# Memory keys and values of the cross attention as split products with rounded operands, the value weights in blocks of 256 outputs

## The chip, the cores and the metric

The kernel runs on one core of a Trainium2 chip. The metric is the device time of one execution in microseconds (us); before and after are compared by the median of several runs. The engines are TensorE (PE, its weight loads PEld), VectorE (DVE), ScalarE (ACT), GpSimd (POOL) and the queue of SyncE (SP), which issues nearly all transfers.

## The reference

Two networks run one after the other on the same 512 tokens of width 1024, all in float32. The first has two hybrid layers (convolution, grouped attention, a gated recurrence, a Fourier mix) and ends with an RMS norm. The second begins with that result as its stream x and has a memory of 256 rows:

```python
x = first_block(...)                                  # 512 x 1024
h = _rms_norm(x, g_mix_pre)
proj = h @ w_in                                       # 22 tiles of 128 columns and a narrow one
...                                                   # window attention, gated delta net, w_out
c = _memory_cross_attention(_rms_norm(x, g_cross_pre), _rms_norm(mem, g_mem), w_cq, w_ckv, w_co)
x = x + _rms_norm(c, g_cross_post)
f = _swiglu(_rms_norm(x, g_ffn_pre), w_gate_up, w_down)
```

The keys and the values of the cross attention are `_rms_norm(mem, g_mem) @ w_ckv`: a 256 x 1024 matrix times 1024 x 1024 for the keys and the same for the values. They don't depend on x, and the kernel computes them between the two networks.

## The kernel before

Activations lie feature-major: tile k of `h` holds features 128 k to 128 k + 127 on the partitions and tokens along the row, 512 latent ones (`LAT`) and behind them 256 (`CTX`) which hold the memory rows (`mem_x`) once the last layer of the first network no longer needs them. All weights stream through a ring of five chunks of 128 x 1024 (`ring`), one transfer each, in one fixed order. A chunk is normally all that one output tile of 128 features needs. A transfer into a place of the ring waits until PE has used the chunk five before it (`chunk_used`).

Nearly every projection is a split product (`project_split`, L1568 to L1589). A weight chunk is rounded to the format fp32r by ACT into one of two buffers (`w_lead`, in the table of names `scratch_r`; L668), then POOL subtracts the rounded part from the chunk in place (L507, `w_split`). The activations are split in the same way (rounded part and rest) by DVE, ACT or POOL. PE then makes three products of rounded operands per tile: first part by first part, first part by rest, rest by first part. ACT may write the rounded part of chunk m only when PE is done with chunk m - 2:

```python
if m >= 2:
    act.wait_ge(chunk_used, SPLIT_STREAM[m - 2] + 1)
```

The memory keys (`ck`) and values (`cv`) are the exception: they are plain float32 products from the raw chunk (`project`, L1551; the loop at L1947 to L1955). A key tile has the weights as the stationary operand and 256 memory rows as the moving one; a value tile has 128 memory rows as the stationary operand and 128 weight columns as the moving one. ACT and POOL have no weights to split in that time.

The order on each engine is that of the program text. Around the change it is:

- the last out projection of the first network (`out1`, 8 tiles) with the residual on DVE (L1215), the memory's RMS norm (L1208) in the middle, and the sums of squares of the final norm (`norm_step`, L1622), which PE makes from squares by ACT (L628);
- ACT issues the transfer of the second table of constants (`const2`) behind the final norm's root, and PE waits for it ahead of `ck`;
- `ck`, 8 tiles. ACT copies each result out (L658). Behind tiles 4 to 7 stand the sums of squares of the norm that opens the second network, two of them each;
- `cv`, 8 tiles. ACT takes the root of that norm behind tile 0 (L622, L623); DVE scales the stream (L1288, 8 operations), ACT rounds each tile (L867) and DVE subtracts (L1293, 8 operations). ACT rounds the first two chunks of `proj_2` behind tile 5;
- DVE computes the angles of the rotary table (`half_turn`, L1267 to L1280), ACT its sine and cosine (L888 to L890). Only then comes ACT's loop over the 22 tiles of `proj_2`, whose first step rounds the chunk of tile 2;
- `proj_2`, 22 tiles of 24 matmuls each on PE. Its tile 0 waits for each activation tile in turn (`x_split`).

## Time and profile before

| | us |
|---|---|
| median of 3 runs | 2168.32 (2159.36 to 2172.3) |
| the profiled execution, as a run | 2171.4 |
| its span in the trace | 2169.6 |

| engine | busy us | share of the span |
|---|---|---|
| PE | 1925.8 | 89% |
| PEld | 1524.1 | 70% |
| DVE | 716.9 | 33% |
| ACT | 683.3 | 31% |
| POOL | 603.3 | 28% |

Matmuls overlap one another in the trace, so the distance between their starts tells what one costs, not its duration. Times in the text such as 1088.19 are microseconds from the start of the span. An f32 matmul of the program shows as two records, an fp32r one as a single record.

### The profile page before, as it was taken

To read this page: it belongs to the slowest core of one execution; us is meant where nothing else is said; L and a number is where in the kernel's file an instruction comes from. 1 tells how busy PE (TensorE), PEld (TensorE's weight loads), DVE (VectorE), ACT (ScalarE), POOL (GpSimd) and SP (SyncE) were. 2 spreads that over 40 slices of the span, in tenths; PEclk is the share of its full clock that TensorE was granted. 3 is DMA by queue.
4 is the path that set the end of the run, shared out by engine and by line. 5 is a ranking of instruction groups with operands and counts; after the bars stand their busy time and mean duration, and the time that the engine had idled before them with its cause. 6 is when DMAs were issued, how large, how long until landed. Compare 5 with 4: busy or idle time off the path is not lost.

```text
span 2169.6 us, 36056 instructions
## 1 busy us (share of the span) xinstructions
PE 1925.8 (89%) x15546; PEld 1524.1 (70%) x15546; DVE 716.9 (33%) x1394; ACT 683.3 (31%) x1092; POOL 603.3 (28%) x319
## 2 busy tenths in 40 slices
PE   6899998777989997878889898888889989999996
PEld 2688884764868874656668677688657858888874
DVE  0300101747341011546312752866431243333101
ACT  3322322015342244015313292700343342222222
POOL 0222225104113333202203230131223424444442
PEclk9999999668989998559999996989999999999998
DMA  8233332000112222100233220000112112233331
GB/s 294 78 115 101 114 127 86 5 3 1 40 39 68 68 88 68 41 2 10 70 106 117 65 82 30 1 3 3 31 47 78 49 49 90 95 97 97 97 97 58
DMA packets 40822, 147.16 MB, mean 68 GB/s; under 512 B 4320, under 2 KB 5472, under 8 KB 40544
## 3 DMA queue, kind: packets, MB, share of 16 engines
q1 hardware_dynamic: 39344, 142.82, 20.3%
q8 instruction: 123, 2.02, 0.4%
q10 hardware_dynamic: 1328, 2.10, 0.3%
q14 instruction: 27, 0.22, 0.0%
HBM read 142.80 MB, written 2.10 MB: 67 GB/s over the span
## 4 chain that ended last, share of the span: by engine, by line
PE 76%; DVE 13%; ACT 6%; issue 3%; DMA 1%; SPq 0%; POOL 0%; DVEq 0%; ACTq 0%
PE wide_ps L1586 50%; PE pair_ps L1622 4%; PE wide_ps L1679 2%; PE duo_ps L1820 2%; PE pair_ps L1694 2%; PE wide_ps L1564 1%; PE wide_ps L1772 1%; PE wide_ps L1954 1%; PE wide_ps L1983 1%; PE pair_ps L2104 1%; PE wide_ps L2101 1%; PE wide_ps L2080 1%; ACT xn L753 1%; PE duo_ps L1605 1%; PE wide_ps L2039 1%
## 5 line engine op out<-in xcount | busy, mean ns | idle before, releaser
L507 POOL TENSOR_TENSOR ring_r<-ring,scratch_r 128x1024 fp32r<-128x1024 f32 x186 | 450.5, 2423 | 1257.6 <-ACT scratch_r L668 1257.6
L1586 PE MATMUL wide_ps<-xn_r,scratch_r 128*128 128x512 f32 (+1 forms) x1424 | 530.6, 373 | 0.0
L1586 PE MATMUL wide_ps<-work_r,scratch_r 128*128 128x512 f32 x1242 | 480.2, 387 | 33.3 <-DVE xn_r L1071 21.9
L1586 PE MATMUL wide_ps<-work_r,ring_r 128*128 128x512 f32 x1242 | 463.5, 373 | 0.0
L668 ACT ACTIVATE scratch_r<-ring 128x1024 fp32r<-128x1024 f32 x186 | 196.8, 1060 | 798.6 <-PE wide_ps L1586 763.8
L1586 PEld LDWEIGHTS wide_ps<-xn_r,scratch_r 128*128 128x128 f32 x1424 | 271.5, 191 | 52.8 <-issue 6.1
L1586 PEld LDWEIGHTS wide_ps<-work_r,scratch_r 128*128 128x128 f32 x1242 | 235.5, 190 | 100.3 <-issue 43.9
L1586 PEld LDWEIGHTS wide_ps<-work_r,ring_r 128*128 128x128 f32 x1242 | 235.4, 190 | 42.8
L1586 PE MATMUL wide_ps<-proj_r,scratch_r 128*128 128x512 f32 x704 | 242.9, 393 | 1.5 <-DVE proj_r L1071 1.5
L1586 PEld LDWEIGHTS wide_ps<-proj_r,scratch_r 128*128 128x128 f32 x704 | 133.2, 189 | 37.4 <-issue 8.7
L1163 DVE SCALAR_TENSOR_TENSOR proj<-proj,par_sb,qe 128x768 f32<-128x768 f32 (+1 forms) x6 | 5.6, 930 | 345.0 <-ACT qe L623 345.0
L1622 PE MATMUL pair_ps<-work,const_sb 128*128 128x512 f32 (+1 forms) x176 | 82.3, 591 | 22.4 <-ACT work L628 22.4
L1510 DVE SCALAR_TENSOR_TENSOR xn<-xn,par_sb,work 128x512 f32<-128x512 f32 x24 | 17.7, 747 | 230.3 <-ACT work L623 230.3
L658 ACT ACTIVATE proj<-wide_ps 128x512 f32<-128x512 f32 (+2 forms) x116 | 73.6, 634 | 62.1 <-PE wide_ps L1564 37.8
L1586 PE MATMUL wide_ps<-proj_r,ring_r 128*128 128x512 f32 x208 | 82.6, 397 | 0.0
L1586 PE MATMUL wide_ps<-conv_tmp_r,scratch_r 128*128 128x512 f32 x198 | 74.2, 375 | 0.8 <-DVE xn_r L1071 0.7
L1622 PEld LDWEIGHTS pair_ps<-work,const_sb 128*128 128x128 f32 x176 | 32.9, 204 | 59.0 <-ACT work L628 37.3
L1586 PE MATMUL wide_ps<-conv_tmp_r,ring_r 128*128 128x512 f32 x198 | 73.7, 372 | 0.0
L1215 DVE TENSOR_TENSOR h<-h,work 128x768 f32<-128x768 f32 (+1 forms) x16 | 34.8, 2173 | 93.9 <-ACT work L794 93.9
L1679 PE MATMUL wide_ps<-xn,proj 64*64 64x32 f32 x1920 | 52.5, 270 | 11.9 <-DVE scratch L1108 7.6
L1679 PEld LDWEIGHTS wide_ps<-xn,proj 64*64 64x64 f32 x1920 | 49.1, 194 | 16.0 <-DVE proj L1103 7.6
L1694 PEld LDWEIGHTS pair_ps<-scratch,work 64*64 64x64 f32 x1920 | 49.2, 199 | 10.1 <-issue 10.1
(358 smaller groups left out, 2765.2 us busy)
## 6 DMA issues: line engine op xcount, KB each, us to landing
ring<-weights SPq DMA_DIRECT2D x260, 512.0 KB, 3.6
h<-tokens SPq DMA_DIRECT2D x4, 768.0 KB, 12.4
out<-h SPq DMA_DIRECT2D x1, 2048.0 KB, 7.3
const_sb<-const SPq DMA_DIRECT2D x1, 1089.0 KB, 7.7
h<-mem ACTq DMA_DIRECT2D x1, 1024.0 KB, 5.9
proj<-const ACTq DMA_DIRECT2D x1, 768.5 KB, 4.4
state<-positions ACTq DMA_DIRECT2D x1, 256.0 KB, 4.7
par_sb<-par SPq DMA_DIRECT2D x1, 128.5 KB, 2.2
```

Source lines behind the costliest of these rows:

```text
L507: pool.tensor_tensor(as_r(wt), wt, as_r(w_lead[:, m % 2, :]).bitcast(F32), ALU.subtract).then_inc(w_split, 1)
L658: act.activation(dst, wide_ps[:, g % 2, 0:w], func).then_inc(evacuated, 1)
L668: act.activation(as_r(w_lead[:, m % 2, :]), ring[:, c % RING, :], ACT.Copy).then_inc(w_lead_ready, 1)
L753: act.activation(pair_probs(p)[:, r * (b - a):(r + 1) * (b - a)], wide_ps[:, r, a:b], ACT.Exp, bias=neg_max[:, m % 4:m % 4 + 1], scale=HD ...
L1215: dve.tensor_tensor(h[:, n, 0:w], h[:, n, 0:w], resid[:, n % 2, 0:w], ALU.add).then_inc(h_ready, 1)
L1564: last = pe.matmul(wide_ps[:, g % 2, a:b], wt[:, k % KT * P:(k % KT + 1) * P], rhs(k)[:, a:b], start=k == 0, stop=k == k_tiles - 1)
L1586: last = pe.matmul(wide_ps[:, g % 2, a:b], wt[:, cols], as_r(x[:, a:b]), start=n == 0 and p == 0, stop=n == len(k_order) - 1 and p == 2)
L1605: last = pe.matmul(mod_row_ps(ly, b)[32 * k:32 * k + 32, :], c_wide[:, 4 * half + k, :], wt[:, k, :], start=half == 0, stop=half == 1, ski ...
L1622: last = pe.matmul(pair_ps[:, a:b], cst["ones"], squares(n)[:, k % 2, a:b], start=k == 0, stop=k == KT - 1)
L1679: last = pe.matmul(score_bank(d, r)[tokens_half, 32 * c:32 * c + 32], hg_k(j, d)[rows, chunk_cols(c, a)], halves(hg_q(j, d)[rows, chunk_co ...
L1694: last = pe.matmul(halves(out_bank(a)[rows, 64 * c:64 * c + 64], 1 << l)[:, :, 1 - d, :], v_tok[tokens_half, j, c, rows], masked(l, d)[tok ...
L1820: last = pe.matmul(ft_bank(s, j)[:, 0:size], ft_buf[:, tt, part * P:(part + 1) * P], wt[:, base + part * size:base + (part + 1) * size], s ...
```

## The change

The keys and values become split products. Their 16 chunks join the list of chunks that ACT rounds and POOL subtracts, between `out1` and `proj_2`. `h` moves into the group of buffers that can also be seen as fp32r, and DVE splits the eight tiles of the normed memory (`memory_split`) into a rounded part (`mem_lead`, in free columns of `xn`) and a rest. A key tile is now 24 matmuls of 256 columns. The values are made in 4 blocks of 256 outputs: a block takes two chunks, each of which holds 4 of the 8 input tiles by 256 outputs, and 48 matmuls of 256 columns whose stationary operand is the memory.

```diff
-    stages = [..., ("out1", KT, KT), ("proj_2", 22, KT),
+    stages = [..., ("out1", KT, KT), ("ck", KT, KT),
+              ("cv", KT, KT), ("proj_2", 22, KT),
...
+        STREAM_SQUARES = {KT - 3: (0, 1), KT - 2: (2, 3), KT - 1: (4, 5), KT: (6, 7)}
+        mem_lead = xn_t[:, :, LAT:TOK]
...
-            split_weights("proj_2")
+            for stage in ("ck", "cv", "proj_2"):
+                split_weights(stage)
...
-                    leads_after(f"out{ly}", n, "proj1" if ly == 0 else None)
+                    leads_after(f"out{ly}", n, ("proj1", "ck")[ly])
...
             for n in range(KT):
+                leads_after("ck", n, "cv")
                 evacuate("ck", n, PLAN["ck"] + n + 1, CTX, key_c[:, n, :])
-                if n >= 4:
-                    for k in (2 * n - 8, 2 * n - 7):
+                for k in STREAM_SQUARES.get(n, ()):
+                    act.wait_ge(scaled, 8 * N_FINAL + k + 1)
+                    square(N_MIX_PRE, k, x_2[:, k, :], LAT)
+            for n in range(KT // 2):
+                g = EVAC["cv"] + n
+                leads_after("cv", 2 * n, "proj_2")
+                leads_after("cv", 2 * n + 1, "proj_2")
+                act.wait_ge(chunk_used, PLAN["cv"] + 2 * n + 2)
+                act.activation(val_c[:, :, 2 * n * P:2 * (n + 1) * P], wide_ps[:, g % 2, :].rearrange("p (t n) -> p t n", t=2)[:, :, 0:2 * P],
+                               ACT.Copy).then_inc(evacuated, 1)
+                if n == 0:
+                    for k in STREAM_SQUARES[KT]:
                         act.wait_ge(scaled, 8 * N_FINAL + k + 1)
                         square(N_MIX_PRE, k, x_2[:, k, :], LAT)
...
-                if n == 0:
+                if n == 1:
                     mean_root(N_MIX_PRE, LAT)
-                if n >= 3:
-                    norm_leads(N_MIX_PRE, (2 * n - 6, 2 * n - 5) if n < 7 else ())
-                if n == KT - 3:
-                    weight_leads("proj_2", 0, 2)
+                if n >= 2:
+                    norm_leads(N_MIX_PRE, range(4 * n - 8, 4 * n - 4))
...
+            def memory_split(k):
+
+                dve.wait_ge(scaled, 8 * N_MEM + k + 1)
+                split(mem_x[:, k, :], mem_lead[:, k, :])
...
                     if ly and n == 4:
                         memory_norm()
+                    if ly and n >= 4:
+                        memory_split(2 * n - 8)
+                        memory_split(2 * n - 7)
...
             def ck(n):
-                project("ck", n, PLAN["ck"] + n, KT, lambda k: mem_x[:, k, :], CTX, scaled_by(N_MEM) if n == 0 else None)
+                project_split("ck", n, range(KT), lambda k: mem_lead[:, k, :], lambda k: mem_x[:, k, :], CTX,
+                              after(X_SPLITS["ck"]) if n == 0 else None)
...
+                for half in range(2):
+                    m = SPLIT_AT["cv"] + 2 * n + half
+                    pe.wait_ge(w_split, m + 1)
...
+                    for i in range(4):
+                        k, cols = 4 * half + i, slice(2 * P * i, 2 * P * i + 2 * P)
+                        for t in range(2):
+                            run = slice(t * P, (t + 1) * P)
+                            for p, (x, wt) in enumerate(((mem_lead[:, k, run], w_first), (mem_x[:, k, run], w_first),
+                                                         (mem_lead[:, k, run], w_rest))):
+                                last = pe.matmul(wide_ps[:, g % 2, 512 * t:512 * t + 2 * P], as_r(x), wt[:, cols],
+                                                 start=k == 0 and p == 0, stop=k == KT - 1 and p == 2)
+                    last.then_inc(chunk_used, 1)
```

ACT, before, from the last `ck` tile to the root of the opening norm (L658 copies a `ck` result out, L628 squares, L878 copies a `cv` result out, L622 and L623 are the root):

```order
L658 ACTIVATE proj<-wide_ps 128x256
L628 ACTIVATE work<-h 128x512 x2
L878 ACTIVATE proj<-wide_ps 128x2x128
L622 ACTIVATE work<-pair_ps,eps 128x512
L623 ACTIVATE work<-work 128x512
```

And right behind it, to the second tile of `proj_2` (L867 rounds activations, L668 rounds a weight chunk, L888 begins the rotary table):

```order
L878 ACTIVATE proj<-wide_ps 128x2x128 x3
L867 ACTIVATE work_r<-xn 128x512 x2
L878 ACTIVATE proj<-wide_ps 128x2x128
L867 ACTIVATE conv_tmp_r<-xn 128x512
L867 ACTIVATE work_r<-xn 128x512
L878 ACTIVATE proj<-wide_ps 128x2x128
L867 ACTIVATE work_r<-xn 128x512 x2
L668 ACTIVATE scratch_r<-ring 128x1024 x2
L878 ACTIVATE proj<-wide_ps 128x2x128
L867 ACTIVATE work_r<-xn 128x512 x2
L878 ACTIVATE proj<-wide_ps 128x2x128
L888 ACTIVATE proj<-proj 128x512
```

ACT, of the changed kernel, from the second `cv` block to the same place (here L672 rounds a weight chunk, L884 copies a block out, L626 and L627 are the root, L871 rounds activations, L896 begins the rotary table):

```order
L884 ACTIVATE proj<-wide_ps 128x2x256
L626 ACTIVATE work<-pair_ps,eps 128x512
L627 ACTIVATE work<-work 128x512
L672 ACTIVATE scratch_r<-ring 128x1024 x2
L884 ACTIVATE proj<-wide_ps 128x2x256
L871 ACTIVATE work_r<-xn 128x512 x2
L871 ACTIVATE conv_tmp_r<-xn 128x512
L871 ACTIVATE work_r<-xn 128x512
L672 ACTIVATE scratch_r<-ring 128x1024 x2
L884 ACTIVATE proj<-wide_ps 128x2x256
L871 ACTIVATE work_r<-xn 128x512 x4
L896 ACTIVATE proj<-proj 128x512
```

The root has moved from behind the first eighth of the values to behind the second quarter, and four of the eight activation tiles are now rounded behind the last copy of the values instead of none.

ACT at the end of `out1`, before (L794 copies a tile out, L859 and L862 issue the two transfers, L658 is the first `ck` result):

```order
L668 ACTIVATE scratch_r<-ring 128x1024
L794 ACTIVATE work<-wide_ps,small 128x512
L628 ACTIVATE work<-h 128x512 x2
L794 ACTIVATE work<-wide_ps,small 128x512
L628 ACTIVATE work<-h 128x512 x2
L794 ACTIVATE work<-wide_ps,small 128x512
L628 ACTIVATE work<-h 128x512 x4
```

And in the changed kernel (L672 rounds a weight chunk, L798 copies a tile out, L632 squares):

```order
L672 ACTIVATE scratch_r<-ring 128x1024
L798 ACTIVATE work<-wide_ps,small 128x512
L632 ACTIVATE work<-h 128x512 x2
L672 ACTIVATE scratch_r<-ring 128x1024
L798 ACTIVATE work<-wide_ps,small 128x512
L632 ACTIVATE work<-h 128x512 x2
L672 ACTIVATE scratch_r<-ring 128x1024
L798 ACTIVATE work<-wide_ps,small 128x512
L632 ACTIVATE work<-h 128x512 x4
```

The chunks of `ck` tiles 0 and 1 are rounded ahead of the copies and squares of the last two `out1` tiles.

## Rows read from the trace of the kernel before

**Rows 1.** The page's chain that ended last, shares of the span by engine.

```profile
PE 76%; DVE 13%; ACT 6%; issue 3%; DMA 1%; SPq 0%; POOL 0%; DVEq 0%; ACTq 0%
```

**Rows 2.** Timeline, `ck` and `cv`: start, duration, engine, line, names, count [idle before].

```profile
1088.19 20.33 PE L1564 MATMUL wide_ps<-h,ring 128*128 128x256 f32 x80 [5.25 <-DMA proj<-const]
...
1121.82 0.39 ACT L658 ACTIVATE proj<-wide_ps 128x256 f32<-128x256 f32 x1 [5.01 <-PE wide_ps L1564]
...
1122.92 1.99 PE L1622 MATMUL pair_ps<-work,const_sb 128*128 128x512 f32 x4 [1.14 <-ACT work L628]
1124.74 3.62 PE L1564 MATMUL wide_ps<-h,ring 128*128 128x256 f32 x16
...
1131.32 28.75 PE L1954 MATMUL wide_ps<-ring,h 128*128 128x128 f32 x256
```

**Rows 3.** Timeline, PE in the first projection: rounded operands, 256 and 512 columns.

```profile
200.24 0.28 PE L1586 MATMUL wide_ps<-conv_tmp_r,scratch_r 128*128 128x256 f32 x1
...
200.59 0.40 PE L1586 MATMUL wide_ps<-work_r,scratch_r 128*128 128x512 f32 x1
```

**Rows 4.** Timeline, the chunk of `proj_2` tile 2 through ACT, POOL and PE.

```profile
1169.11 1.05 ACT L668 ACTIVATE scratch_r<-ring 128x1024 fp32r<-128x1024 f32 x1
1170.24 2.36 POOL L507 TENSOR_TENSOR ring_r<-ring,scratch_r 128x1024 fp32r<-128x1024 f32 x1 [9.39 <-ACT scratch_r L668]
...
1170.79 0.40 PE L1586 MATMUL wide_ps<-work_r,ring_r 128*128 128x512 f32 x1
1171.30 1.06 ACT L668 ACTIVATE scratch_r<-ring 128x1024 fp32r<-128x1024 f32 x1 [0.66 <-PE wide_ps L1586]
1172.74 0.47 PE L1586 MATMUL wide_ps<-work_r,scratch_r 128*128 128x512 f32 x1 [1.55 <-POOL ring_r L507]
```

**Rows 5.** Timeline, end of `out1`: ACT with and without a chunk to round.

```profile
1059.09 1.06 ACT L668 ACTIVATE scratch_r<-ring 128x1024 fp32r<-128x1024 f32 x1 [3.95 <-PE wide_ps L1586]
1060.05 0.67 ACT L794 ACTIVATE work<-wide_ps,small 128x512 f32<-128x512 f32 x1
...
1061.38 1.96 PE L1622 MATMUL pair_ps<-work,const_sb 128*128 128x512 f32 x4 [2.39 <-ACT work L628]
...
1068.94 0.69 ACT L794 ACTIVATE work<-wide_ps,small 128x512 f32<-128x512 f32 x1 [7.18 <-PE wide_ps L1586]
...
1070.20 1.99 PE L1622 MATMUL pair_ps<-work,const_sb 128*128 128x512 f32 x4 [1.29 <-ACT work L628]
```

**Rows 6.** Timeline, DVE and POOL operations that meet.

```profile
1158.03 2.82 POOL L507 TENSOR_TENSOR ring_r<-ring,scratch_r 128x1024 fp32r<-128x1024 f32 x1
1158.54 2.85 DVE L1293 TENSOR_TENSOR xn_r<-xn,work_r 128x512 fp32r<-128x512 f32 x1
...
1196.46 2.40 POOL L507 TENSOR_TENSOR ring_r<-ring,scratch_r 128x1024 fp32r<-128x1024 f32 x1 [3.15 <-ACT scratch_r L668]
1196.90 2.51 DVE L1310 TENSOR_TENSOR proj<-proj 128x512 f32<-128x512 f32 x1
```

**Rows 7.** Timeline, from the root of the opening norm to the rotary table.

```profile
1135.37 0.68 ACT L622 ACTIVATE work<-pair_ps,eps 128x512 f32<-128x512 f32 x1
1136.74 2.08 DVE L1288 SCALAR_TENSOR_TENSOR xn<-h,par_sb,work 128x512 f32<-128x512 f32 x3 [47.00 <-ACT work L623]
...
1165.87 0.63 ACT L888 ACTIVATE proj<-proj 128x512 f32<-128x512 f32 x1 [5.39 <-DVE proj L1280]
```

**Rows 8.** Windows: us, PE, PEld, DVE, ACT, POOL busy (x), PEclk, DMA share, GB/s.

```profile
1050.00:1088.00 38.00, 27.96 (x103) 18.62 (x101) 14.57 (x19) 10.33 (x16) 5.79 (x3) 0.99 0.25 83
...
1083.00:1087.00 4.00, 0.00 (x0) 0.00 (x0) 2.64 (x4) 1.29 (x2) 0.00 (x0) 1.00 0.51 188
1089.00:1093.00 4.00, 4.00 (x10) 3.15 (x10) 0.75 (x2) 0.00 (x0) 0.00 (x0) 0.50 0.00 0
1094.00:1098.00 4.00, 4.00 (x21) 3.52 (x20) 0.00 (x0) 0.39 (x1) 0.00 (x0) 1.00 0.42 131
...
1236.00:1240.00 4.00, 3.83 (x7) 2.44 (x8) 3.43 (x6) 0.00 (x0) 0.00 (x0) 0.50 0.00 0
```

More of the change, by code:

```diff
@@ L1942, in _ @@
                 ck(n)
[L1943 to L1944 removed]
+                for k in STREAM_SQUARES.get(n, ()):
+                    if k == 0:
                         pe.wait_ge(root_ready, N_FINAL + 1)
[L1946 to L1956 removed]
+                    norm_step(N_MIX_PRE, k, LAT)
+            for n in range(KT // 2):
+                cv(n)
+                if n == 0:
+                    for k in STREAM_SQUARES[KT]:
+                        norm_step(N_MIX_PRE, k, LAT)
             for t in range(22):
```

43 lines of the change are left out of this document (15 added, 28 removed).

## The prediction

> **What bounds the kernel now.** I first read the page's chain: 76% of it is PE, 13% DVE, 6% ACT [rows 1]. So PE sets the end except in places where it waits. Then I read the timeline where the change sits. PE starts `ck` at 1088.19 after 5.25 us of waiting for the constants, and a key tile costs 3.45 us once the clock is up (16 records in 3.62 us, less 0.17 us by which the last one's end overlaps what follows) [rows 2]. Behind tile 5, 6 and 7 PE idles 1.14 us until ACT has copied and squared, then makes two sums in 1.99 us. The values take 28.75 us without a gap, 3.58 us a chunk [rows 2]. PE is thus the bound in `ck` and `cv`, POOL is idle there, and ACT nearly so.
>
> What comes behind `cv` is not PE's. The last subtraction of the opening norm on DVE starts at 1158.54 and lasts 2.85 us, to 1161.39 [rows 6]. Then DVE makes the angles and hands them to ACT at 1165.87 [rows 7]; ACT rounds the chunk of tile 2 only behind the table, at 1169.11, POOL subtracts at 1170.24, and PE, idle for 1.55 us, starts tile 2 at 1172.74 [rows 4]. So from that last subtraction to tile 2 there are 1172.74 - 1161.39 = 11.35 us that no matmul shortens, and this chain already sets PE's time before the change. **Tile 2 of `proj_2` is the place at which the change is to be judged.**
>
> **What the matmuls give.** Three rounded matmuls of 256 columns start from 200.24 on and the next one of 512 at 200.59 [rows 3]: 0.117 us each. A chunk of 24 is 2.80 us, and its last record ends 2.96 us after its start. Against 3.45 and 3.58 us this is 0.65 us for each of 8 key chunks and 0.78 us for each of 8 value chunks: 11.4 us, if nothing else had to keep up.
>
> **What the chunks now need first.** A rounded chunk can be begun only when PE has finished the chunk two before it. From rows 4: PE ends 1170.79 + 0.40 = 1171.19, ACT starts 1171.30, so 0.11; ACT start to POOL start 1.13; POOL 2.36; POOL end to PE start 0.14. Sum 3.74 us. Two chunks therefore take at least 2.96 + 3.74 = 6.70 us, or 3.35 us each, wherever PE does nothing in between: of the 0.65 us only 0.10 is left, of the 0.78 only 0.23.
>
> Before `ck`, ACT rounds two more chunks ahead of the copies and squares of the last two `out1` tiles. ACT's start-to-start for one is 1060.05 - 1059.09 = 0.96 us, and PE there waits for the squares (1.29 us idle) [rows 5]. That is twice 0.96, so PE, the root, the transfer of the constants and the start of `ck` come 1.95 us later, at 1090.14. The 16 memory operations on DVE lie beside this: the seventh and eighth residual may be held up by POOL, but the last square, due at 1083.1, needs the last residual only by then, and I get 1082.9. I cost them at nothing; were this cover gone, each 0.1 us late is 0.1 us on the path. The waiting for weights of `ck` 0 and 1 is covered by `out1`.
>
> **Walking PE through, on the axis of the trace before.** After the wait the clock is at its lower level of 1.2 GHz until between 1093 and 1094, some 5.2 us after the restart [rows 8]; I keep 5.2 us, in which 22 rounded matmuls fit. Chunk 0 ends 1095.7, chunk 1 starts at once and ends 1098.5. Then by the rule of 3.74: chunk 2 starts 1099.45, 3 at 1102.25, 4 at 1106.15, 5 at 1108.95, end 1111.9. Behind 5, 6 and 7 ACT first rounds a chunk (0.11 + 0.96), then copies and squares (1121.82 to 1122.92, 1.10 us [rows 2]): PE idles 2.2 us instead of 1.14, and the sums take 1.8 to the next tile. This gives chunk 6 at 1115.9, 7 at 1122.85, and the first value chunk at 1129.8, against 1131.32 before, but with two of the sums still to come. Value chunks 0 and 1 end 1132.75 and 1135.55; the sums cost 2.4 + 1.8 us; chunk 2 starts 1139.75, 3 ends 1145.5; 4 starts 1146.45, 5 ends 1152.2, 6 starts 1153.6, and the last ends about 1159.5. Against 1160.07 that is a gain of only 0.6 us at the end of `cv`.
>
> **What is late.** The root now stands behind the second block: ACT starts it at 1147.15 and DVE its first scaling at 1148.55 (1.37 us later, as 1135.37 to 1136.74 [rows 7]), 11.8 us later than before. The rounding of activations waits for the third block's copy, 1153.9. From here DVE and POOL meet. The rows show what that costs: a DVE operation of 0.69 us that comes 0.44 us after POOL's start lasts 2.51 us, to 0.55 us behind POOL's end; and POOL's 2.40 us becomes 2.82 when DVE is in the way [rows 6]. They take turns. The first subtraction is ready at 1154.5, but POOL has chunk 7 until 1155.85, so it ends 1156.4. Twelve DVE operations follow (5 scalings, 7 subtractions; 0.68 us each, 8.2 us), and the first two chunks of `proj_2` fall in between (4.8 us): the last subtraction ends at 1156.4 + 13.0 = 1169.4. Before it was 1161.39. ACT has no longer wait than that: its last rounding comes right behind the last scaling.
>
> The Trainium skill, "SBUF — State Buffer", section "Who interferes with whom", states that a DVE instruction with two SBUF inputs and a GpSimd instruction that reads SBUF exclude each other for the whole instruction. By that rule both orders of arrival cost what the two pairs above show, so the trace agrees. If they ran side by side, the twelve operations would end at about 1164.4, and tile 2 would be 3.0 us late instead of 8.0.
>
> Tile 2 is 11.35 us behind that: 1180.75 against 1172.74, **+8.0 us**. Behind it everything (copies, the convolution on DVE from tile 6 on, PE) hangs on PE's tiles and moves as a whole.
>
> **The clock.** PE starts tile 0 at about 1161.7 and takes its eight activation tiles as DVE gives them, to 1170.2; tile 1 ends 1175.8; then it idles 5.0 us. In the trace before, a wait of 5.25 us (1083 to 1088) was followed by 1.2 GHz in 1089 to 1093, and the wait of 8.7 us that ends at 1236 by 1.2 GHz to 1240 [rows 8]. About 4.8 to 5.2 us at half speed cost 2.4 to 2.6 us, none of it if the clock falls earlier, in the thin stretch of tile 0, and is back up by tile 2. I take the row nearest to 5.0 us of idling, so +2.4.
>
> The sum: 8.0 + 2.4 = +10.4 us. The profiled execution took 2171.4 us (span 2169.6), 3.1 above the median of 2168.3; I add to the median: **2178.7 us**, +0.48%. About 0.5% (10.8 us) is also what a measurement of this kernel can tell from no change.
>
> **The rivals.**
> 1. *The weights keep up and PE sets the time.* Then 11.4 - 1.95 = 9.5 us are won: 2158.8 us. For it speaks that POOL's 2.36 us is less than a chunk's 2.80. Against it: the chunks go through ACT, POOL and PE in series over two buffers, and tile 2 hangs on the angles. It decides only if PE's end to the start two chunks on is under 2.7 us, not 3.74, and the last subtraction ends before 1161.4. Chance 0.06.
> 2. *DVE and POOL hardly meet* (the operations fall between one another): +3.0, the clock stays up because PE hardly idles: 2171.3 us. The rows show two meetings of two possible. Chance 0.09.
> 3. *As forecast, but tile 2 finds the clock up*, since it fell and rose in tile 0 and 1 under cover of the wait: +8.0, 2176.3 us. For it: PE is busy for about half of 8 us in tile 0. Chance 0.25.
> 4. *The forecast*, 2178.7 us. Chance 0.42. Its own range is 2175 to 2182.
> 5. *The clock falls in `ck` and `cv` too.* There PE idles 2.2 us in every 7.0 behind chunk 5, 6, 7 and the first block. Each fall costs up to 2.5 us, and one or two make +13 to +16: 2181 to 2184 us. Against it: in the last tiles of `out1` PE idled 2.39 and 1.29 us in front of the sums [rows 5], and the window from 1050 to 1088 shows a clock of 0.99 [rows 8]. Chance 0.18.
>
> **How the numbers follow.** The range takes in rivals 2 to 5 and about 2 us for the scatter of the median (the three runs before lie 13 us apart): 2170 to 2187. Below it lies rival 1. The line at +10.8 us cuts the forecast in two nearly equal parts. Slower by over 0.5%: half of 0.42, nearly all of 0.18, a little of rival 3, 0.39. Faster by over 0.5%: rival 1 without the part within the line, 0.06. The rest, 0.55, is within 0.5%.
>
> **What would show it.** In the profile after: 24 records of 256 columns 0.117 us apart in each chunk; PE waiting for POOL ahead of chunks 2 and 4 of `ck` by 0.8 to 1.0 us, two chunks in 6.7 us; `ck` starting 1.9 us later; squares 2.2 us behind tiles 5 to 7; `cv` ending within 1.5 us of 1160; the first scaling near 1148.6 and the last subtraction near 1169.4, with subtractions of 2 us and more; ACT's wait for the angles about 8 us later; tile 2 near 1180.8 after some 5 us of idling, and its first 5 us at 1.2 GHz. The prediction is wrong if the last subtraction comes before 1165, if PE's period in `ck` is under 3 us, or if the clock is low in `cv`.

## The result and the profile after

| | before | after |
|---|---|---|
| median, us | 2168.24 (10 runs, 2159.36 to 2173.31) | 2178.97 (10 runs, 2175.66 to 2184.34) |
| the profiled execution, as a run | 2171.4 | 2181.97 |
| its span | 2169.6 | 2180.2 |

The ratio of the medians is 1.0053, 95% interval 1.0037 to 1.0069: 10.7 us slower, where the prediction said 10.4. The page gives PE 75%, DVE 14% and ACT 6% of the chain that ended last, hardly another picture than [rows 1]. The difference is to be looked for in one stretch.

Timeline of the kernel after, PE, from the last sums of the final norm to tile 2 of `proj_2` (start, duration, engine, line, names, count, idle before and its releaser):

```profile
1063.58 1.96 PE L1638 MATMUL pair_ps<-work,const_sb 128*128 128x512 f32 x4 [2.39 <-ACT work L632]
...
1083.24 5.55 PE L1638 MATMUL pair_ps<-work,const_sb 128*128 128x512 f32 x8 [2.30 <-ACT work L632]
1094.03 0.58 PE L1602 MATMUL wide_ps<-xn_r,scratch_r 128*128 128x256 f32 x1 [5.24 <-DMA proj<-const]
...
1102.14 0.36 PE L1602 MATMUL wide_ps<-xn_r,scratch_r 128*128 128x256 f32 x1 [0.93 <-POOL ring_r L510]
...
1109.00 0.36 PE L1602 MATMUL wide_ps<-xn_r,scratch_r 128*128 128x256 f32 x1 [0.92 <-POOL ring_r L510]
...
1117.20 3.62 PE L1638 MATMUL pair_ps<-work,const_sb 128*128 128x512 f32 x4 [2.25 <-ACT work L632]
...
1125.83 1.98 PE L1638 MATMUL pair_ps<-work,const_sb 128*128 128x512 f32 x4 [2.14 <-ACT work L632]
...
1151.19 0.36 PE L1968 MATMUL wide_ps<-scratch_r,xn_r 128*128 128x256 f32 x1 [0.94 <-POOL ring_r L510]
...
1166.11 0.47 PE L1602 MATMUL wide_ps<-work_r,scratch_r 128*128 128x512 f32 x1 [2.08 <-ACT proj L884]
...
1184.43 0.77 PE L1602 MATMUL wide_ps<-work_r,scratch_r 128*128 128x512 f32 x1 [4.57 <-POOL ring_r L510]
1185.00 0.63 PE L1602 MATMUL wide_ps<-xn_r,scratch_r 128*128 128x512 f32 x1
1185.42 0.63 PE L1602 MATMUL wide_ps<-work_r,ring_r 128*128 128x512 f32 x1
...
1249.97 2.05 PE L2000 MATMUL pair_ps<-proj,const_sb 128*128 128x512 f32 x2 [8.68 <-DVE proj L1327]
```

Against [rows 2], where 80 records of a key tile's form and 256 of a value tile's run without a gap, the reader sees a wait for POOL in front of every second chunk, 6.86 us apart (1102.14 to 1109.00), and in front of the sums a wait of 2.1 to 2.3 us instead of 1.14. The wait of 1.55 us ahead of tile 2 [rows 4] is now 4.57 us, and the rows behind it are 0.43 us apart instead of 0.23.

The view of waits sums them up, PE from 1080 to 1190 (microseconds in total, times, longest):

```profile
PE pair_ps L1638 <- ACT work L632: 11.0, 5, 2.3
PE wide_ps L1602 <- POOL ring_r L510: 6.4, 3, 4.6
PE wide_ps L1602 <- DMA proj<-const: 5.2, 1, 5.2
PE wide_ps L1602 <- ACT proj L884: 2.1, 1, 2.1
PE wide_ps L1968 <- POOL ring_r L510: 2.0, 2, 1.1
PE wide_ps L1602 <- DVE xn_r L1309: 1.6, 3, 1.0
```

and the same view of the kernel before, 1078 to 1178:

```profile
PE pair_ps L1622 <- ACT work L628: 6.0, 5, 1.3
PE wide_ps L1564 <- DMA proj<-const: 5.2, 1, 5.2
PE wide_ps L1586 <- POOL ring_r L507: 1.6, 1, 1.6
```

PE waits 28.3 us instead of 12.8. The 15.5 us between them are more than the 11.4 us that the prediction has the matmuls give.

Behind `cv`, the timeline of the kernel after on ACT, DVE and POOL:

```profile
1151.79 0.68 ACT L626 ACTIVATE work<-pair_ps,eps 128x512 f32<-128x512 f32 x1
...
1153.16 2.59 DVE L1304 SCALAR_TENSOR_TENSOR xn<-h,par_sb,work 128x512 f32<-128x512 f32 x3 [57.56 <-ACT work L627]
...
1163.62 5.19 POOL L510 TENSOR_TENSOR ring_r<-ring,scratch_r 128x1024 fp32r<-128x1024 f32 x2 [2.92 <-ACT scratch_r L672]
1163.71 2.84 DVE L1304 SCALAR_TENSOR_TENSOR xn<-h,par_sb,work 128x512 f32<-128x512 f32 x1
1166.48 2.89 DVE L1309 TENSOR_TENSOR xn_r<-xn,work_r 128x512 fp32r<-128x512 f32 x1
1171.22 1.88 DVE L1309 TENSOR_TENSOR xn_r<-xn,work_r 128x512 fp32r<-128x512 f32 x3
...
1177.59 0.63 ACT L896 ACTIVATE proj<-proj 128x512 f32<-128x512 f32 x1 [5.63 <-DVE proj L1296]
...
1180.83 1.04 ACT L672 ACTIVATE scratch_r<-ring 128x1024 fp32r<-128x1024 f32 x1
1181.94 4.67 POOL L510 TENSOR_TENSOR ring_r<-ring,scratch_r 128x1024 fp32r<-128x1024 f32 x2 [13.13 <-ACT scratch_r L672]
```

The chain is that of [rows 7] and [rows 4], later: root, scalings and subtractions, angles, table, chunk, tile 2. Two DVE operations of 0.7 us meet POOL's two chunks and last 2.84 and 2.89 us.

Windows of the kernel after (columns as in [rows 8]):

```profile
1083.00:1088.00 5.00, 4.76 (x7) 1.95 (x8) 3.33 (x5) 1.96 (x4) 1.52 (x1) 0.66 0.18 70
...
1180.00:1184.00 4.00, 0.00 (x0) 0.00 (x0) 0.00 (x0) 3.86 (x6) 2.06 (x1) 0.77 0.44 133
1184.00:1190.00 6.00, 5.57 (x15) 4.46 (x16) 0.00 (x0) 0.00 (x0) 2.61 (x2) 0.58 0.00 0
```

PE idles from 1180 to 1184 and begins tile 2 at 1.2 GHz. What was not in the prediction is the first of the three windows: the clock also fell in the final norm's sums, whose eight records took 5.55 us instead of 3.89, 1.66 us more.

**A measure for the experiments.** PE waits 8.7 us for the convolution in every kernel of this case, and everything that the change touches from the end of `out1` to there lies between two rows: the first sums with a wait of 2.39 us, and the first sums behind the wait of 8.68. For the kernel before they are the 1061.38 of [rows 5] and

```profile
1236.17 2.05 PE L1973 MATMUL pair_ps<-proj,const_sb 128*128 128x512 f32 x2 [8.68 <-DVE proj L1311]
```

which makes 174.79 us; after it is 1249.97 - 1063.58 = 186.39. The difference is 11.60 us, of which 1.66 are the fall of the clock in the final norm's sums. The spans differ by 10.6: ahead of the stretch the kernel after is 2.2 us later (the profiles of this case lie 5.1 us apart there, 1058.48 to 1063.58), and behind it 3.2 us shorter. I call this **the stretch**. It comes from one execution, whose clock also falls by chance, so it stands beside the medians and not in their place. Behind the stretch the kernels do the same work, but what remains there varies from 928.3 to 934.2 us over the fourteen profiles of this case.

### The profile page after: what moved, and what is told of

It reads as the page before. It is cut to its first block, busy times and chain, and to the rows that moved or that the text cites. A ratio compares the mean times of both kernels' runs of the same rounds, so it can differ in the third digit from the quotient of the medians.

```text
span 2180.2 us, 36108 instructions
## 1 busy us (share of the span) xinstructions
PE 1924.9 (88%) x15546; PEld 1521.9 (70%) x15546; DVE 727.4 (33%) x1410; ACT 698.2 (32%) x1104; POOL 640.7 (29%) x335
## 4 chain that ended last, share of the span: by engine, by line
PE 75%; DVE 14%; ACT 6%; issue 3%; DMA 1%; POOL 0%; SPq 0%; DVEq 0%; ACTq 0%
PE wide_ps L1602 50%; PE pair_ps L1638 3%; PE wide_ps L1695 2%; PE pair_ps L1710 2%; PE duo_ps L1836 2%; PE wide_ps L1788 2%; PE wide_ps L2010 1%; ACT xn L757 1%; PE pair_ps L2131 1%; PE wide_ps L2128 1%; PE wide_ps L2107 1%; PE duo_ps L1621 1%; PE wide_ps L2066 1%; DVE xn L1241 1%; DVE xn L1304 1%
## 5 line engine op out<-in xcount | busy, mean ns | idle before, releaser
L510 POOL TENSOR_TENSOR ring_r<-ring,scratch_r 128x1024 fp32r<-128x1024 f32 x202 | 487.9, 2416 | 1232.2 <-ACT scratch_r L672 1232.2
L1602 PE MATMUL wide_ps<-xn_r,scratch_r 128*128 128x512 f32 (+1 forms) x1488 | 551.9, 371 | 7.1 <-DMA proj<-const 5.2
L672 ACT ACTIVATE scratch_r<-ring 128x1024 fp32r<-128x1024 f32 x202 | 213.8, 1060 | 861.9 <-PE wide_ps L1602 811.4
L1602 PEld LDWEIGHTS wide_ps<-xn_r,scratch_r 128*128 128x128 f32 x1488 | 284.8, 191 | 62.0 <-issue 9.1
L1558 DVE TENSOR_TENSOR proj<-proj,state 128x512 f32<-128x512 f32 x11 | 27.7, 2520 | 82.6 <-ACT state L662 82.6
```

What stands on the lines that cost most here:

```text
L510: pool.tensor_tensor(as_r(wt), wt, as_r(w_lead[:, m % 2, :]).bitcast(F32), ALU.subtract).then_inc(w_split, 1)
L672: act.activation(as_r(w_lead[:, m % 2, :]), ring[:, c % RING, :], ACT.Copy).then_inc(w_lead_ready, 1)
L1558: dve.tensor_tensor(tile_2[:, t, :], tile_2[:, t, :], up_2[t % 2], ALU.mult).then_inc(ffn_ready, 1)
L1602: last = pe.matmul(wide_ps[:, g % 2, a:b], wt[:, cols], as_r(x[:, a:b]), start=n == 0 and p == 0, stop=n == len(k_order) - 1 and p == 2)
```

## The experiments

Eleven kernels, one of them run twice, in three groups; each group has its own runs of the kernel before on its chip (medians 2170.44 us of 35 runs, 2169.24 of 19, 2171.28 of 19; 2168.24 beside the changed kernel). So a difference between two medians of different groups holds up to 3 us of the chips. A difference of two ratios, times 2170 us, takes that out; it stands below as "by the ratios", and is known to about 4 us. The theory to be tested: the loss has three parts, the chain ACT, POOL, PE over two buffers for rounded chunks; ACT's roundings ahead of squares and root, which delay the opening norm and with it the angles; and the slow clock behind the wait for tile 2. The last column is the part of the stretch from PE's first record of `ck` on; it leaves out the final norm's sums, in which the clock fell in some executions.

| kernel | edit to the changed kernel | median | ratio to before, 95% interval | stretch | from `ck` on |
|---|---|---|---|---|---|
| before | | 2168.24 | | 174.79 | 147.98 |
| after | | 2178.97 | 1.0053 (1.0037 to 1.0069) | 186.39 | 155.94 |
| e1_early | sums, root, roundings earlier | 2174.94 | 1.0019 (1.0005 to 1.0032) | 183.16 | 154.31 |
| e2_angles | angles ahead of the scaling | 2172.59 | 1.0011 (0.9996 to 1.0027) | 179.54 | 149.31 |
| e5_keep_clock | 18 idle matmuls ahead of tile 2 | 2175.33 | 1.0021 (1.0008 to 1.0033) | 182.92 | 154.09 |
| e6_three | third buffer | 2170.02 | 0.9999 (0.9984 to 1.0014) | 174.58 | 147.85 |
| e3_keys_only | keys alone split | 2172.49 | 1.0012 (1.0002 to 1.0023) | 179.84 | 147.74 |
| e4_values_only | values alone split | 2176.53 | 1.0038 (1.0023 to 1.0053) | 177.82 | 150.98 |
| e7_both | e1 and e2 | 2176.78 | 1.0040 (1.0026 to 1.0055) | 183.17 | 152.84 |
| e12_both_again | the same once more | 2177.63 | 1.0035 (1.0022 to 1.0048) | 182.34 | 153.57 |
| e11_root_early | e7, roundings as in after | 2176.03 | 1.0023 (1.0015 to 1.0032) | 179.44 | 150.68 |
| e9_all | e1, e2 and e6 | 2161.19 | 0.9966 (0.9953 to 0.9979) | 170.02 | 143.23 |
| e10_three_angles | e2 and e6 | 2160.45 | 0.9953 (0.9941 to 0.9966) | 167.14 | 140.33 |
| e8_before_angles | kernel before, angles earlier | 2166.03 | 0.9973 (0.9960 to 0.9985) | 174.35 | 146.16 |

### Angles ahead of the scaling

```diff
+            half_turn()
             dve.wait_ge(root_ready, N_MIX_PRE + 1)
             scale_and_split(N_MIX_PRE, "g_mix_pre")
-            half_turn()
```

> The changed kernel with one edit: DVE computes the rotary angles ahead of the opening norm's scaling, in the time in which it idles, instead of behind the last subtraction. Theory A: ACT's table begins right behind its last rounding, 5.6 us earlier, tile 2 of proj_2 is released about 1.1 us before PE ends tile 1, the wait of 4.57 us and the slow clock behind it (2.2 us) go: 6 to 7 us under the changed kernel, 2172 to 2173 us. Rival B: no change, 2179 us. Rival C: only if the wait goes, with 2.2 of it from the clock.

Measured: 2172.59 us, 6.4 under the changed kernel as expected; by the ratios 9. In its timeline ACT comes to the table right behind its last rounding, and no row of tile 2 has a wait:

```profile
1166.12 1.88 DVE L1309 TENSOR_TENSOR xn_r<-xn,work_r 128x512 fp32r<-128x512 f32 x3
...
1166.77 0.61 ACT L896 ACTIVATE proj<-proj 128x512 f32<-128x512 f32 x1
...
1169.99 1.04 ACT L672 ACTIVATE scratch_r<-ring 128x1024 fp32r<-128x1024 f32 x1
```

Eight DVE operations on 128x512 that need nothing but the positions stood on the path, behind a norm that they don't use. In the changed kernel the rounding for tile 2 starts 7.73 us behind the end of the last subtraction (1180.83 less 1171.22 + 1.88), here 1.99 us behind it (1169.99 less 1166.12 + 1.88). The wait of 4.57 us and the slow clock behind it are both gone. From the start of `ck` to the convolution it is 149.31 us instead of 155.94, 6.6 less, which is 4.57 and 2.2 nearly.

### The third buffer

Columns 6144 to 7167 of `proj`, free at that time, serve as a third place for the rounded chunks of `ck` and `cv`.

```diff
-                    if m >= 2:
-                        act.wait_ge(chunk_used, SPLIT_STREAM[m - 2] + 1)
-                    act.activation(as_r(w_lead[:, m % 2, :]), ring[:, c % RING, :], ACT.Copy)...
+                    if lead_before(m) is not None:
+                        act.wait_ge(chunk_used, SPLIT_STREAM[lead_before(m)] + 1)
+                    act.activation(as_r(lead_at(m)), ring[:, c % RING, :], ACT.Copy)...
```

> The changed kernel with a third buffer for the rounded chunks of keys and values (in columns of proj that are free then), so that ACT and POOL can be three chunks ahead; the order on every engine stays. Theory A (PE's end, ACT, POOL and PE in series over two buffers, 3.74 us, is what holds two chunks at 6.7 to 6.9 us): PE no longer waits for POOL ahead of chunks 2 and 4 of the keys and 4 and 6 of the values (0.93, 0.92, 0.94, 1.06 us), a chunk takes 2.8 us throughout, the sums start some 1.2 instead of 2.2 us behind their tile; values end and root start 7 to 9 us earlier; about 2170 to 2172 us. Rival: POOL's 2.4 us and ACT's 1 us per chunk are what holds it: the period stays above 3.2 us and under 2 us are won, 2177 to 2179 us.

Measured: 2170.02 us, 9.0 under the changed kernel; by the ratios 11.7, and the stretch is 11.8 us shorter. Its timeline shows no wait for POOL in `ck` and `cv`, the waits ahead of the sums back to those of before, and tile 2 still waiting:

```profile
1068.45 1.98 PE L1651 MATMUL pair_ps<-work,const_sb 128*128 128x512 f32 x4 [1.30 <-ACT work L645]
...
1107.45 1.96 PE L1651 MATMUL pair_ps<-work,const_sb 128*128 128x512 f32 x4 [1.23 <-ACT work L645]
...
1167.98 0.77 PE L1615 MATMUL wide_ps<-work_r,scratch_r 128*128 128x512 f32 x1 [4.55 <-POOL ring_r L523]
```

A third buffer takes away two costs at once: ACT can round a chunk before PE has finished the one two back, and so the rounding is already done when the tile's copy and squares are due. The tail from the last subtraction to tile 2 is a separate cost: 4.55 us of waiting against 4.57. Tile 2 itself starts 81.61 us behind the start of `ck` (1167.98 less 1086.37) and not 90.40: the chain hangs on the root, and the root on PE's sums.

### Sums, root and roundings earlier

The sums stand behind key tiles 4 to 7, the root behind the first block of values, ACT's roundings of activations behind blocks 1 and 2 (counted from 0) instead of 2 and 3.

```diff
-        STREAM_SQUARES = {KT - 3: (0, 1), KT - 2: (2, 3), KT - 1: (4, 5), KT: (6, 7)}
+        STREAM_SQUARES = {KT - 4: (0, 1), KT - 3: (2, 3), KT - 2: (4, 5), KT - 1: (6, 7)}
...
-                if n == 1:
+                if n == 0:
                     mean_root(N_MIX_PRE, LAT)
-                if n >= 2:
-                    norm_leads(N_MIX_PRE, range(4 * n - 8, 4 * n - 4))
+                if n in (1, 2):
+                    norm_leads(N_MIX_PRE, range(4 * n - 4, 4 * n))
```

> The changed kernel with the sums of squares back behind key tiles 4 to 7, the root behind the first value block and the activations rounded behind the second and third block. Theory A (the end is set by the chain root, 16 DVE operations, angles, table, chunk of tile 2): the root comes 9 to 10 us earlier, the last subtraction ends before the last value block, PE waits under 2 us ahead of tile 2 of proj_2 and its clock stays up; 2165 to 2169 us, 10 to 12 us under the changed kernel. Rival B (the split products and their chunks cost the time themselves, wherever the norm stands): no more than 2 us are won, about 2177 us. Rival C (only falls of the clock cost): about 2.2 us are won.

Measured: 2174.94 us, 4 us under the changed kernel and not 10 to 12: a miss (by the ratios 7.4). The timeline, and two windows (columns as in [rows 8]):

```profile
1159.96 0.36 PE L1964 MATMUL wide_ps<-scratch_r,xn_r 128*128 128x256 f32 x1 [2.11 <-POOL ring_r L510]
...
1166.82 2.62 DVE L1285 CAST proj<-state 128x512 f32<-128x512 int32 x1
...
1135.00:1140.00 5.00, 5.00 (x19) 3.77 (x20) 0.00 (x0) 0.32 (x1) 1.29 (x1) 0.66 0.12 50
1160.00:1165.00 5.00, 5.00 (x30) 5.00 (x31) 5.00 (x5) 1.27 (x3) 2.60 (x1) 0.66 0.17 68
```

The last subtraction ends at 1166.88, 3.8 us earlier if both are counted from the start of `ck` (75.24 us against 79.07), and PE waits only 0.33 us ahead of tile 2, with the clock up. So far the theory holds. But tile 2 starts no earlier, 90.84 us behind the start of `ck` against 90.40: now PE itself is late, since tile 0 starts 5.5 us later than in the changed kernel (77.61 us against 72.08). Two new costs appear. ACT, in the order of the text, rounds activations ahead of two weight chunks, and PE waits 2.11 us instead of about 1 for the last pair of chunks. And the angles, once earlier, run into POOL, which has chunks of `proj_2` to subtract: the cast at their head, 0.42 us in the trace of the kernel before, lasts 2.62. The other part of the 5.5 us is the clock: it is low for some 3.4 us in each of the two windows (0.66 of full speed over 5 us), which costs about 1.7 us each time. In the changed kernel's profile it was up there; of the kernel with the same order and the angles moved (below) one execution (e7) has it down near both places and the other (e12) has it up. So this part is not shown to come from the order. What the stretch of e1 has gained, 3.2 us, is the clock at tile 2 (63.47 us from there to the convolution instead of 65.54) and the final norm's sums, which ran at the high clock here.

### Keeping PE busy ahead of tile 2

Eighteen float32 matmuls of constants, whose result nobody reads, in the place of the wait.

```diff
+                if t == 2:
+                    for _ in range(18):
+                        pe.matmul(duo_ps[:, 0:P], cst["ones"], cst["ident"], start=True, stop=True)
                 project_split("proj_2", t, range(KT), ...
```

> The changed kernel with 18 small extra matmuls (128 columns, f32, results unused, some 3.9 us) ahead of tile 2 of proj_2, where PE otherwise idles 4.57 us. Theory A says the chain through DVE, ACT and POOL releases tile 2 at the same moment, and that 2.2 us of the loss are the slow clock behind the wait: the first matmuls of tile 2 start 0.23 us apart instead of 0.43, and the time is 1.5 to 2.2 us under the changed kernel, about 2177 us. A rival in which PE's own work sets the time would be 3.9 us slower, 2183 us.

Measured: 2175.33 us, 3.6 under the changed kernel (by the ratios 6.9), more than the term of 2.4 us. Timeline:

```profile
1175.12 4.18 PE L2004 MATMUL duo_ps<-const_sb 128*128 128x128 f32 x36
...
1179.88 0.47 PE L1602 MATMUL wide_ps<-work_r,scratch_r 128*128 128x512 f32 x1 [0.58 <-POOL ring_r L510]
```

Tile 2's first record now takes 0.47 us and not 0.77: the clock is up. From the rows after, 4.4 us at half speed (1184.43 to about 1188.8) cost 2.2 us. The two traces bear that out: tile 2 is released at the same moment (90.67 us behind the start of `ck` against 90.40), and from its first record to the convolution it is 63.42 us instead of 65.54, 2.1 less. What the medians show beyond that lies within what they leave open.

### One part of the change alone

With the keys alone, the values stay float32 products in 8 tiles as before, and the sums stand behind key tiles 4 to 7:

```diff
-            for stage in ("ck", "cv", "proj_2"):
+            for stage in ("ck", "proj_2"):
                 split_weights(stage)
...
-            for n in range(KT // 2):
-                cv(n)
+            for n in range(KT):
+                wt = use_chunk(PLAN["cv"] + n)
...
+                        last = pe.matmul(wide_ps[:, g % 2, t * P:(t + 1) * P], as_r(mem_x[:, k, t * P:(t + 1) * P]).bitcast(F32),
```

With the values alone, sums, root and roundings stand as in the run above, and no chunk is rounded at the end of `out1`:

```diff
-            for stage in ("ck", "cv", "proj_2"):
+            for stage in ("cv", "proj_2"):
                 split_weights(stage)
...
-                project_split("ck", n, range(KT), lambda k: mem_lead[:, k, :], lambda k: mem_x[:, k, :], CTX,
+                project("ck", n, PLAN["ck"] + n, KT, lambda k: as_r(mem_x[:, k, :]).bitcast(F32), CTX,
```

> Only the keys as split products; the values are the plain float32 products of before in 128 columns, with the order of before on ACT and PE (sums behind key tiles 4 to 7, root behind the first value tile). They are made from the remainder part of the memory alone, so the output is not the reference's; the instructions and sizes are those of before. Theory A: two more chunks to round in front of the last copies of the out projection (1.95 us), the sums' wait longer by 1 us behind four tiles, one tenth won per key tile, and nothing changed behind the values: 3 to 5 us above the kernel before, 2172 to 2175 us; tile 2 of proj_2 waits 1.5 us for its chunk as before. Rival (the key products themselves are cheaper and nothing else counts): 5 us under the kernel before, 2164 us.

> Only the values as split products in blocks of 256 outputs, with the order of e1_early behind them; the keys are the plain float32 products of before, from the remainder part of the memory alone, so the output is not the reference's. The first two value chunks are rounded behind key tiles 6 and 7. Theory A: 2 us from the longer wait for the squares behind key tiles 6 and 7, some 2 us from value chunks that wait for POOL, some 2 us from the collisions of DVE and POOL between the last value chunk and tile 2: 3 to 6 us above the kernel before, 2173 to 2176 us. Rival (the value products are cheaper and nothing else counts): 6 us under the kernel before, 2163 us.

Measured: 2172.49 us with the keys alone, as expected, and 2176.53 with the values alone (five runs), half a microsecond above what was expected: by the ratios +2.6 and +8.2 us. Neither part pays. Their sum of 10.8 us looks like the changed kernel's +11.5, but it is not that loss taken apart: both have the sums and the root early, and the kernel with both parts in that order is e1, at +4.1 us by its ratio. The traces don't add up to the medians either: the stretch of the keys alone is 5.05 us longer than before, 3.3 of them falls of the clock at the end of `out1`, and from the start of `ck` on 0.2 us shorter; that of the values alone is 3.03 us longer. So I read no more from these two than that each is slower than the kernel before.

### All edits together, and the two that matter

> e1_early and e2_angles together: sums and root earlier, angles ahead of the scaling. Theory A: nothing of the chain root, scaling, angles, table reaches beyond PE's end of tile 1, so tile 2 of proj_2 no longer waits for its chunk, and what is left is the series of ACT, POOL and PE per chunk: 3 to 5 us under e1_early, 2169 to 2172 us, about level with the kernel before. Rival (the two edits remove the same wait, so one of them is enough): no faster than e2_angles, 2172.6 us.

> e7_both with the third buffer of e6_three. Theory A: the three parts of the loss (two buffers, late root, angles behind the last subtraction) are gone, and the gain of the products remains: about 9 us under e7_both, 2160 to 2163 us, 7 to 10 us under the kernel before (the 11.4 us of the products, less the collisions). Rival (DVE and POOL together become the bound behind the values): no more than 3 us under e6_three, 2167 us.

Measured: 2176.78 us without the third buffer, a miss by nearly 5 us, above the 2172.59 of the angles alone; 2161.19 us with it, as expected. The order that had looked like a gain made things worse beside the early angles. So the next group took it apart, repeated it and left it out. Apart from the edits shown, e11 differs from e7 in this:

```diff
-                if n in (1, 2):
-                    norm_leads(N_MIX_PRE, range(4 * n - 4, 4 * n))
+                if n >= 2:
+                    norm_leads(N_MIX_PRE, range(4 * n - 8, 4 * n - 4))
```

> The run of early sums, early root and early angles once more, with nothing changed: whether its 2176.8 us from five executions holds. If the order itself loses, 2175 to 2178 us again; if those executions were out of line, 2170 to 2173.

> The run of early sums, early root and early angles, except that ACT rounds the activations behind blocks 2 and 3 of the values, as the changed kernel does, and not behind blocks 1 and 2, where they stood ahead of the rounding of two weight chunks. That run took 2176.8 us, the angles alone 2172.6. If the miss of the former came from ACT rounding activations ahead of weight chunks (2.1 us of PE's wait ahead of the last value chunks, and a late first chunk of proj_2), this one comes to 2169 to 2173 us. If it came from the clock (a stretch at the lower level at the start of ck, where both have the same order), it stays at 2175 to 2178.

> The changed kernel with the third buffer for rounded chunks (alone 2170.0 us) and the angles ahead of the scaling (alone 2172.6), sums and root where the change has them. Of the third buffer's run PE still idled 4.55 us ahead of tile 2 of proj_2, so the angles should give 4.5 us and perhaps 2 us of slow clock: 2163.5 to 2165.5 us. All three edits together gave 2161.2. Theory A (sums and root earlier are worth 2 to 4 us once the weights keep up): this run 2 to 4 us above the run of all three. Theory B (the earlier sums and root only move waits about and are worth nothing): within 1.5 us of 2161.2.

The repeat gave 2177.63 us: the miss is real. Its timeline around the end of `cv`:

```profile
1158.54 0.64 ACT L871 ACTIVATE work_r<-xn 128x512 fp32r<-128x512 f32 x1 [2.84 <-DVE xn L1300]
...
1160.35 1.99 ACT L672 ACTIVATE scratch_r<-ring 128x1024 fp32r<-128x1024 f32 x2
1161.47 4.68 POOL L510 TENSOR_TENSOR ring_r<-ring,scratch_r 128x1024 fp32r<-128x1024 f32 x2 [4.17 <-ACT scratch_r L672]
...
1163.92 0.77 PE L1598 MATMUL wide_ps<-work_r,scratch_r 128*128 128x512 f32 x1 [3.40 <-issue]
```

ACT waits 2.84 us for a scaling on DVE (which waits for POOL), with the first two chunks of `proj_2` behind it in its queue. They are rounded at 1160.35, and PE idles 3.40 us (the trace names no releaser; POOL's first chunk ends just before) ahead of tile 0 and begins it at 1.2 GHz (first record 0.77 us). With the roundings back where the changed kernel has them, PE waits there for 2.21 us with the clock up, and the stretch is 2.9 us shorter (179.44 against 182.34). The median fell by 1.6 us only, to 2176.03 (by the ratios 2.6), inside the range that was expected if the clock and not ACT's order were the cause. But in e12's own trace the eight sums of the final norm ran at the high clock (3.89 us), and the miss was there all the same. ACT's order explains part of it, 2.9 us in these two executions; what makes up the rest is not shown. The early sums themselves bring nothing. In the changed kernel the last two sums stand behind block 0 and their wait of 2.21 us takes the place of a wait for POOL; behind key tile 4 they add one. The timeline of e11 has five waits for POOL in `ck` and `cv` where that of e2 has four. Between e11 and e2 lie 3.4 us by the medians and 2.6 by the ratios. Their stretches are equal (179.44 and 179.54), but that of e2 has a fall of the clock in the final norm's sums in it (3.42 us for four), which that of e11 has not; from the start of `ck` on e11 takes 150.68 us and e2 149.31. So 1.4 us are seen in the traces, and the rest stays open.

Without the early order and with the third buffer the kernel took 2160.45 us, 3 to 5 us under what was expected, and its stretch is 2.9 us shorter than with that order. Theory A, by which the earlier sums and root were worth 2 to 4 us, falls; theory B, that they are worth nothing, holds. It is the best of all: 0.9953 of the time before, 18.5 us under the changed kernel (by the ratios 21.7). Its waits, PE from 1080 to 1180:

```profile
PE wide_ps L1615 <- DMA proj<-const: 5.3, 1, 5.3
PE pair_ps L1651 <- ACT work L645: 4.7, 4, 1.2
PE wide_ps L1615 <- issue: 2.1, 1, 2.1
PE wide_ps L1615 <- DVE xn_r L1322: 0.3, 1, 0.3
```

12.4 us of waiting, as in the kernel before, none of it for POOL. Its two rows of the stretch:

```profile
1061.57 1.96 PE L1651 MATMUL pair_ps<-work,const_sb 128*128 128x512 f32 x4 [2.40 <-ACT work L645]
...
1228.71 2.04 PE L2013 MATMUL pair_ps<-proj,const_sb 128*128 128x512 f32 x2 [8.68 <-DVE proj L1340]
```

167.14 us against 174.79 before: 7.65 us are won here. Not all of that is the products'. The early angles also take away the 1.55 us that the kernel before waited for tile 2, and the next experiment gives them to the kernel before alone.

### The angles in the kernel before

The edit of the first experiment, in the kernel before.

> The kernel before, with the angles of the rotary table ahead of the scaling of the stream. PE idled 1.55 us ahead of tile 2 there, so at most 1.5 us can be won: 0 to 1.5 us under the kernel before. If it wins 3 us or more, the angles cost something else than that wait, and the gain of 6.4 us that they gave the changed kernel would not be read from the wait ahead of tile 2 alone.

Measured: 2166.03 us, 0.9973 of the kernel before on that chip: 5.3 us less (the interval of the ratio is 3.3 to 8.7), where at most 1.5 was expected. The stretch fell from 174.79 to 174.35 us; from the start of `ck` (1090.25) to the end of the stretch (1236.41) it is 146.16 against 147.98, which is the wait for tile 2 (1.55) and a little. Of its profile's 4.9 us of shorter span, 5.1 lie behind the stretch. The windows there, before and then e8:

```profile
1400.00:1480.00 80.00, 70.69 (x1908) 69.33 (x1906) 55.76 (x106) 8.61 (x28) 25.50 (x20) 0.89 0.01 3
```

```profile
1400.00:1480.00 80.00, 69.54 (x2048) 68.05 (x2047) 56.68 (x104) 7.74 (x26) 25.51 (x20) 0.96 0.01 3
```

In the same 80 us PE gets through 2048 records and not 1908, at a clock of 0.96 instead of 0.89. The work there is the same. Where the falls of the clock land in the recurrence moves the whole by some microseconds, whatever the kernel: from the end of the stretch to the first sums behind the recurrence it is 298.78 us before and 293.96 in e8, but also 297.77 and 294.63 in e7 and e12, which are one program. Whether the edit moves the falls for good or these eight executions were lucky stays open. It also says that the 6.4 us of the angles in the changed kernel need not all be the wait ahead of tile 2; there, however, the stretch itself is 6.85 us shorter.

This kernel is the fair measure for the best one, since both have the angles early and both ran on one chip. 2160.45 us against 2166.03 is 5.6 us less, and from the start of `ck` to the convolution 140.33 against 146.16 is 5.8. So of the 11.4 us that the prediction has the matmuls give, some 5.8 arrive even with a third buffer; 2.1 more go into a wait ahead of tile 0 that the kernel before does not have. The other part of what the best kernel gains on the kernel before, the early angles gave that kernel too, whatever its cause, and it has nothing to do with the split products.

## Why the prediction was right

Both traces are put on one axis by the start of `ck`, which the prediction had at 1090.14 and the trace after has at 1094.03 (3.89 later, of which 2.2 were there before the site: the sums of 1061.38 in [rows 5] stand at 1063.58).

- **What bounds the kernel.** Right: tile 2 decided. With the angles moved alone, 6.4 us came back though not one matmul changed, and with the third buffer alone tile 2 came 8.8 us earlier behind the same wait.
- **The start of `ck`.** Two roundings ahead of two pairs of squares: 1.95 us forecast (twice the 0.96 of the row would be 1.92). The two waits are 2.30 us each against 1.29 and 1.30, and in e11, whose final norm's sums all ran at the high clock, the first sums and `ck` lie 28.76 us apart (1059.11 to 1087.87) against 26.81 before: 1.95. The memory's split on DVE was free, as forecast. In the profiled execution 1.66 us came on top, the eight sums at the low clock (5.55 us against 3.89).
- **Two chunks in 6.70 us.** 6.86 measured, with waits of 0.93 and 0.92 us.
- **The waits ahead of the sums**, 2.2 us: 2.25, 2.14 and 2.21.
- **The root** at 1147.15: 1151.79 less 3.89 is 1147.90. Two errors cancel here, by luck. After the restart I had chunk 2 start 9.31 us behind the start of `ck`; it took 8.11, since the clock rose after 2.7 us and not after 5.2. And four sums behind key tile 5 ran at 1.2 GHz, 3.62 us for 1.98.
- **The last subtraction** at 1169.4: 1171.22 + 1.88 less 3.89 is 1169.21. From the late root to there it took 21.31 us and not 22.25, which makes up for the root. The meetings of DVE and POOL were 2.84 and 2.89 us long, as in [rows 6]. The Trainium skill, "SBUF — State Buffer", section "Who interferes with whom", calls the pair of ports that the two engines share an exclusive lock. These rows agree: a DVE operation that meets POOL ends behind POOL's chunk, in turns.
- **Tile 2** at 1180.75: 1184.43 less 3.89 is 1180.54, with 11.33 us from the last subtraction against 11.35. PE idled 4.57 us, not 5.0.
- **The slow clock**, 2.4 us: 4.4 us at half speed are 2.2 us.
- **The sum**, +10.4: 10.7 by the medians, 11.60 in the stretch of the profiled execution, 9.9 without the fall in the final norm's sums. The mechanism is shown; that the sum fits to 0.3 us is luck, as the interval of the ratio reaches 3.5 us to either side.

Of the rivals, the second and the third are excluded by the rows above (DVE and POOL met; tile 2 began at 1.2 GHz in the execution that was profiled, and e5 takes that cost away). The fifth was half there: the clock did fall in the final norm's sums and behind key tile 5, but the first fall was paid once and the second was made up by the earlier rise, so the time is the fourth's. The first, PE as the bound, is nearest to what the third buffer and the early angles make of the same matmuls. That their 2160.45 us lies close to its 2158.8 is luck: with the angles moved the kernel before took some 5 us less too. What the prediction did not see is how cheaply the loss could be had back. It took the two buffers and the order of the angles as given.

The shares of the loss, as far as they are known: by the ratios the third buffer gives back 11.7 us, the angles 9.1, both 21.7; in the stretch 11.8, 6.9 and 19.3. Within the noise the two add up, so they are separate costs. (The bare medians, 9.0, 6.4 and 18.5, seem to say that both together give more than the sum; they come from three chips.) Both together are more than the change lost, since the products' gain then shows, and with it the wait of 1.55 us for tile 2 that the kernel before had.

## What to carry to other kernels

A product that is split into rounded parts needs its weights prepared in series, and with two buffers the period of two tiles is one tile on PE plus the whole preparation: add that up from rows (here 2.96 + 3.74 us for two chunks of 2.80) before counting the matmuls' gain, and look for a third place first. When an edit beside the change helps, give it to the kernel before as well, or its gain is credited to the change. On engines that run in the order of the text, look behind the last operation of a late chain for work that needs none of it, and put it ahead. And don't move work earlier on an engine for its own sake: earlier sums and roundings only stood in front of chunks that PE needed sooner.

## What was not expected of the hardware

The clock falls at shorter waits than I had taken as harmful, and not every time. Behind waits of 2.30 us the final norm's last eight sums took 5.47 us in e7 and 3.89 in e12, two executions of one program; behind a wait of 2.39 to 2.40 us its first four took 3.44 us in e8 and 1.96 in the kernel before. Behind the wait of 2.25 us ahead of the first sums in `ck` four took 3.20 to 3.65 us in seven of eight profiles (1.96 in e7); in the three kernels with the third buffer that wait is 1.23 us, and they took 1.95 or 1.96. The Trainium skill, "TensorE: Matmul & The Clock Gate", Part 1, says of a kernel's start that the number of matmuls at the lower clock differs from run to run of the same kernel; e7 and e12 show such a difference in the middle of one.

What such falls cost is a few microseconds here and there, up to the 6 us by which the remainders behind the stretch differ; the intervals of the ratios reach some 3 us to either side, so an edit of 2 us can't be told from none in this kernel.
